# Gate and up matrices of the first block's experts: from 8 KB runs, 1 MiB a transfer, to 16 KB runs, 2 MiB a transfer

## The reference, cut to what matters

```python
def ec_moe(h, router_w, router_b, w_gate, w_up, w_down):
    ...
    gate, idx = lax.top_k(jnp.swapaxes(aff, 1, 2), cap)      # cap = 2 * 256 / 16 = 32
    xg = h[bidx, idx]
    hid = jax.nn.silu(jnp.einsum("becd,edf->becf", xg, w_gate)) * jnp.einsum("becd,edf->becf", xg, w_up)
    y = jnp.einsum("becf,efd->becd", hid, w_down) * gate[..., None].astype(h.dtype)
    return jnp.zeros_like(h).at[bidx, idx].add(y)
```

## Time and profile before

| | |
|---|---|
| profiled execution | 1881.59 us |
| its span | 1879.7 us, mean granted TensorE clock 0.851 |
| PE busy | 1450.5 us (77%), 11264 matmuls |
| PE weight loads busy | 738.8 us (39%) |
| VectorE / ScalarE busy | 432.2 us (23%) / 231.3 us (12%) |
| moved by DMA | 638.02 MB, mean 339 GB/s |
| packets of the queue that SP orders on (q1) | 101040, 623.76 MB |
| gate, up and down transfers | 128 each, 1024 KB, median 18.0, 18.5 and 18.1 us from order to landing |

### The profile page before, as it was taken

How to read it: one execution, slowest core, us unless ns; L and a number is a source line. 1 busy time by engine, 2 the same in 40 slices (tenths; PEclk the granted TensorE clock), 3 DMA queues, 4 the chain that set the end, 5 groups by cost and what they waited for, 6 DMA issues and landing times.

```text
span 1879.7 us, 26140 instructions
## 1 busy us (share of the span) xinstructions
PE 1450.5 (77%) x11264; PEld 738.8 (39%) x11264; DVE 432.2 (23%) x966; ACT 231.3 (12%) x480; POOL 25.7 (1%) x46
## 2 busy tenths in 40 slices
PE   5989866777766667879676666666799985899996
PEld 3834432323332233445332322222246643555553
DVE  1472211104000022534100001000115453311112
ACT  2111100001000020422000000000122232100001
POOL 1000000000000000000000000000020000000000
PEclk8988787878887778888777878787799998899998
DMA  9697999999999983857999999999932302599995
GB/s 376 224 367 301 417 421 421 421 421 421 421 420 422 420 333 112 342 223 300 422 421 421 420 420 422 420 420 422 416 136 82 135 12 101 219 421 420 421 421 224
DMA packets 104811, 638.02 MB, mean 339 GB/s; under 512 B 10524, under 2 KB 10524, under 8 KB 42240
## 3 DMA queue, kind: packets, MB, share of 16 engines
q1 hardware_dynamic: 101040, 623.76, 81.4%
q0 software_dynamic: 3664, 12.64, 1.9%
HBM read 635.30 MB, written 1.96 MB: 339 GB/s over the span
## 4 chain that ended last, share of the span: by engine, by line
DMA 50%; PE 40%; DVE 5%; ACT 2%; issue 1%; SPq 0%; DVEq 0%; ACTq 0%
PE ps L1834 38%; DMA ring<-in_moe_w_up 31%; DMA ring<-in_moe_w_down 16%; DMA ring<-in_ada_w 3%; PE ps L1837 2%; ACT work L2130 1%; DMA ring<-in_moe_w 1%; DVE x L2371 1%; DVE tmp L2369 1%; SPq L280 0%; ACT tmp L2130 0%; ACT hT L2130 0%; ACT xn L2130 0%; DVE work L620 0%; DVE work L617 0%
## 5 line engine op out<-in xcount | busy, mean ns | idle before, releaser
L1834 PE MATMUL ps<-ring,work 128*32 128x256 f32 (+3 forms) x7760 | 821.1, 473 | 300.5 <-DMA ring<-in_moe_w_up 107.5
L1834 PEld LDWEIGHTS ps<-ring,work 128*32 128x32 f32 (+2 forms) x7760 | 339.6, 132 | 761.9 <-issue 219.5
L2130 ACT ACTIVATE work<-ps 128x256 f32<-128x256 f32 (+3 forms) x188 | 89.0, 478 | 1278.7 <-PE ps L1834 1017.0
L1834 PE MATMUL ps<-work 32*128 32x256 f32 (+6 forms) x1034 | 143.2, 467 | 17.4 <-ACT work L2130 15.6
L2504 DVE TENSOR_TENSOR work<-work,ps 128x256 f32<-128x256 f32 x32 | 13.5, 421 | 590.0 <-ACT work L2130 590.0
L1834 PEld LDWEIGHTS ps<-work 32*128 32x128 f32 (+3 forms) x1034 | 86.0, 213 | 72.5 <-issue 50.3
L1834 PE MATMUL ps<-ring,condT 128*32 128x512 f32 x576 | 83.6, 712 | 21.9 <-DMA ring<-in_ada_w 13.7
L1834 PE MATMUL ps<-ring,hT 128*128 128x512 f32 (+1 forms) x224 | 97.1, 597 | 2.4 <-issue 1.3
L1837 PE MATMUL ps<-const,work 128*128 128x128 f32 (+1 forms) x394 | 67.0, 302 | 23.6 <-ACT work L2130 7.3
L1834 PE MATMUL ps<-work,xn 128*128 128x128 f32 (+2 forms) x416 | 69.5, 320 | 7.0 <-DVE work L1672 6.8
L1837 PEld LDWEIGHTS ps<-const,work 128*128 128x128 f32 (+1 forms) x394 | 49.4, 166 | 58.5 <-issue 24.0
(11 more groups left out here) (300 smaller groups left out, 680.9 us busy)
## 6 DMA issues: line engine op xcount, KB each, us to landing
ring<-in_moe_w_gate SPq DMA_DIRECT2D x128, 1024.0 KB, 18.0
ring<-in_moe_w_up SPq DMA_DIRECT2D x128, 1024.0 KB, 18.5
ring<-in_moe_w_down SPq DMA_DIRECT2D x128, 1024.0 KB, 18.1
ring<-in_moe_w SPq DMA_DIRECT2D x102, 1024.0 KB, 10.7
ring<-in_ada_w SPq DMA_DIRECT2D x72, 1024.0 KB, 11.1
ring<-in_w_in SPq DMA_DIRECT2D x10, 1024.0 KB, 18.1
ring<-in_fc_w_in SPq DMA_DIRECT2D x6, 1024.0 KB, 27.1
ring<-in_attn_w_qkv SPq DMA_DIRECT2D x6, 1024.0 KB, 18.2
```

What stands on the lines that cost most here:

```text
L1834: return pe.matmul(out, lhsT, rhs, start=start, stop=stop, skip_group_check=True)
L2130: return nc.scalar.activation(out, in_, f, **kw)
```

## The change

Two gate pieces (or two up pieces) that hold the four rows of the same half become one transfer. It writes both neighbouring slots, 16 KB in one run for each partition, and adds 16 to the semaphore of the first slot alone. An expert's first eight pieces are now two gate pieces, two up, two gate, two up, in place of gate and up by turns. SP waits for the second slot of the pair to be free before it orders. TensorE waits once for a pair, then runs 32 matmuls and still counts `piece_used` after each 16. `loaded` counts only the transfers that really write to a slot's semaphore. The number of matmuls, their shapes and the sum's order of rows stay. Down pieces and all other pieces are as they were.

```diff
+        def second_of_pair(n):
+            return any(n0 <= n < n0 + 12 * E and (n - n0) % 12 in (1, 3, 5, 7) for n0 in (P_MOE_A, P_MOE_B))
         def loaded(pe, n, rounds=0):
-            pe.wait_ge(S(f"loaded{n % SLOTS}"), 16 * (n // SLOTS + 1) + 16 * rounds)
+            transfers = sum(not second_of_pair(m) for m in range(n % SLOTS, n + 1, SLOTS))
+            pe.wait_ge(S(f"loaded{n % SLOTS}"), 16 * (transfers + rounds))
...
+        def pair(n):
+            return ring[:, n % SLOTS:n % SLOTS + 2, :].rearrange("p a (k f) -> p (a k) f", k=2)
+        def load_pair(sp, n, src):
+            sp.dma_start(pair(n), src).then_inc(S(f"loaded{n % SLOTS}"), 16)
...
-                        order = [w[s][:, 0, kp // 2, 2 * (kp % 2):2 * (kp % 2) + 2, :] for kp in range(4) for s in range(2)]
-                        order += [down[:, 0, kp] for kp in range(4)]
-                        for j, src in enumerate(order):
-                            n = n0 + 12 * u + j
+                        for q in range(2):
+                            for s in range(2):
+                                n = n0 + 12 * u + 4 * q + 2 * s
+                                place_free(sp, n + 1, BODY * i)
+                                load_pair(sp, n, w[s][:, 0, q])
+                        for kp in range(4):
+                            n = n0 + 12 * u + 8 + kp
                             place_free(sp, n, BODY * i)
-                            load(sp, n, src)
+                            load(sp, n, down[:, 0, kp])
...
                         for s in range(2):
-                            loaded(pe, n + 2 * kp + s)
-                            w = slot(n + 2 * kp + s).rearrange("p (k f) -> p k f", k=2)
-                            for kk in range(2):
+                            m = n + 4 * q + 2 * s
+                            loaded(pe, m)
+                            for kk in range(4):
                                 for j in range(4):
                                     last = mm(ps[32 * j:32 * j + 32, 4 + s, 0:SEQ],
-                                              xe[:, c % 2, 2 * kp + kk, CAP * u:CAP * u + CAP],
-                                              w[:, kk, SEQ * j:SEQ * j + SEQ],
-                                              kp == 0 and kk == 0, kp == 3 and kk == 1)
-                            last.then_inc(S("piece_used"), 1)
+                                              xe[:, c % 2, 4 * q + kk, CAP * u:CAP * u + CAP],
+                                              pair(m)[:, kk, SEQ * j:SEQ * j + SEQ],
+                                              q == 0 and kk == 0, q == 1 and kk == 3)
+                                if kk % 2:
+                                    last.then_inc(S("piece_used"), 1)
```

More of the change, by code:

```diff
@@ L2053, in experts @@
                         pe.wait_ge(S("spread_ready"), layer * E + e)
-                    for kp in range(4):
-                        if e == 0 and kp == 0:
+                    for q in range(2):
+                        if e == 0 and q == 0:
                             pe.wait_ge(S("xe_dve"), 28 * layer + 4)
-                        if e == 0 and kp == 2:
+                        if e == 0 and q == 1:
                             pe.wait_ge(S("xe_act"), 4 * layer + 4)
-                        if e and u == 0 and kp == 0:
+                        if e and u == 0 and q == 0:
                             pe.wait_ge(S("xe_dve"), 28 * layer + 4 + 8 * c)
                         for s in range(2):
-                            loaded(pe, n + 2 * kp + s)
-                            w = slot(n + 2 * kp + s).rearrange("p (k f) -> p k f", k=2)
-                            for kk in range(2):
+                            m = n + 4 * q + 2 * s
+                            loaded(pe, m)
+                            for kk in range(4):
                                 for j in range(4):
                                     last = mm(ps[32 * j:32 * j + 32, 4 + s, 0:SEQ],
-                                              xe[:, c % 2, 2 * kp + kk, CAP * u:CAP * u + CAP],
-                                              w[:, kk, SEQ * j:SEQ * j + SEQ],
-                                              kp == 0 and kk == 0, kp == 3 and kk == 1)
-                            last.then_inc(S("piece_used"), 1)
+                                              xe[:, c % 2, 4 * q + kk, CAP * u:CAP * u + CAP],
[3 more added lines that the diff above has]
+                                    last.then_inc(S("piece_used"), 1)
                     if e == 1:
```

## The result

The changed kernel takes 1868.78 us (median of 7 runs, 1862.7 to 1870.21). The kernel before takes 1877.36 us beside it (7 runs, 1873.12 to 1882.1). The ratio is 0.9946, 95% interval 0.9932 to 0.9961: a gain of half a per cent, small but clear of the noise. The medians are 8.6 us apart, the ratio says 10.1 us. Forecast were 8.8 us less and 1870.2 us.

A forecast was written before the change was run, and what follows sets the result against it. Both expert stages were taken as bound by one queue's stream of 384 weight transfers of 1 MiB, TensorE waiting. Gain 10.3 - 0.5 (starts) - 1.0 (ends) = 8.8 us, from 1879.0 to 1870.2 us; range 1864.5 to 1880.5.

The forecast's parts named there:

- Part 1, run length: Gate and up stream of both expert stages: 16 KB runs save 82 ns a pair, 10.3 us over 126 pairs.
- The completion packets' 9 ns a pair: Gate and up pairs: one completion packet per DMA engine in place of two, priced at 9 ns a pair.
- Part 2, depth: Weight queue inside the expert stages: later pair orders leave it unbroken, margin 4.4 us, cost 0 us.
- Part 3, the starts: Starts of both expert stages: later pair order costs 0 to 1.5 us in stage B, 0.5 taken; nothing in stage A.
- the second dip: Start of stage B, about 886.5 us: a dip in the stream that the delayed pairs were to fill.
- Part 4, the ends: Ends of both stages: 32 matmuls instead of 16 after the last up landing; 0.5 us lost in each.
- The run isn't 16 KB: Rival, gate and up transfers: the run is cut again at 8 KB; 1879.4 us, chance 0.15 shared with "its length no longer counts".
- its length no longer counts: Rival, gate and up transfers: rate near flat beyond 8 KB runs; 1879.4 us, chance 0.15 shared with "The run isn't 16 KB".
- The fixed time is smaller: Rival, weight stream: a packet's fixed time is smaller, as by the skill's 3 cycles; gain 4.0 - 1.5, 1876.5 us, chance 0.12.
- The dry queue: Rival, after each expert's hidden-state chain: queue runs dry while SP waits for the second down slot; 1889 us, chance 0.06.
- the slow long packet: Rival, gate and up pairs: 16 KB packets slow as in the instruction queue; up to 500 us more, chance 0.04.
- stretches outside them move: Sign, outside the expert stages: if the time there changes, the prediction is wrong; no size given.

The follow-up runs named there:

- experiment 1: The changed kernel's 2 MiB gate and up pairs, but each partition's part in two runs of 8 KB; 1875.7 us, ratio 0.9995 to the kernel before.
- experiment 2: The kernel before, 1 MiB transfers, but gate and up rows taken crosswise in runs of 4 KB, not 8 KB; 1896.5 us, ratio 1.0125 to the kernel before.
- experiment 7: The changed kernel, but each order in the expert stages waits for two more used pieces, as if six slots; 1875.4 us, ratio 0.9999 to the kernel before.
- Experiment 5: The changed kernel, but first and last expert of both stages take gate and up in single 1 MiB transfers; 1868.1 us, ratio 0.9958 to the kernel before.
- kernel 9: The changed kernel itself, unaltered, measured again beside the kernel before; 1868.3 us, ratio 0.9951.
- experiment 8: The changed kernel, but each pair ordered as two 1 MiB transfers of 64 partitions, 16 KB runs kept; 2686.4 us, ratio 1.4157 to the kernel before.

## Why the prediction was right, point by point

**Part 1, run length: right.** 82 ns a pair were forecast, 73 of them for the runs. The stream shows 76 and 67 against the kernel before, 78 and 67 against experiment 1, mean 72; from landing to landing it is 75. Per packet the step from 4 to 8 KB was read as 9.1 ns; experiment 2 gives 8.8 to 9.3 for that step, the changed kernel against experiment 1 gives 9.0 to 9.4 for the step to 16 KB. The completion packets' 9 ns a pair are not there: experiment 1 has 2048 fewer, and its 4 MiB take the same 9.94 to 9.95 us. The forecast of 10.3 us stands against 9.4 us between the changed kernel's stages and experiment 1's.

**Part 2, depth: right, too cautious.** No gap opened; in experiment 7, with six slots in place of eight, a stage under way lost 0.7 to 1.0 us.

**Part 3, the starts: right place, size off.** 0.5 us taken, between 0 and 1.5; by the bytes it is 1.0 us (0.42 MB not moved before the first matmul of stage B). I thought that the delayed pairs would fill the second dip. The dip was too shallow for that: in the earlier trace rows its four slices, 0.325 us each, are 7, 7, 5 and 7 tenths busy, which leaves some 0.4 us idle (an estimate from that row) for a delay of 1.5 us.

**Part 4, the ends: wrong sign.** A cost of 1.0 us was taken for both. Stage A's end is unchanged at 12.8 us, so the waits cover the second half of the pair there. Stage B's is 1.8 us shorter, since the last down piece and the scatter ran at full clock (1342.03 follows a block of 64 matmuls without a wait; in the earlier trace rows the last 16 took 1.94 us). The prediction reckoned that the pieces behind the pair might fall to the half clock, not that the pair might keep them at the full one. Experiment 5 takes the pair away from the end and gets the 14.6 us back, and the other profiles agree.

**The sum.** 10.3 - 0.5 - 1.0 = 8.8; the stages show 8.5 us, the medians 8.6, the ratios of two measurements 10.1 and 9.2. The main term is right, but that the sum comes within 0.3 us is luck. By place, the 8.5 us are 8.4 in the two streams, 1.8 gained at the end of stage B and 1.8 lost before expert 1's first landing, its offset of one piece taken off (0.1 in stage A, 1.7 in B; 0.8 and 1.2 in kernel 9). The forecast had 9.7 us for the 118 pairs of the streams, 1.0 lost at the ends, and before expert 1's first landing a gain of 0.2 (0.7 from eight pairs, less 0.5 for the starts). These terms are off by 1.2, 2.8 and 2.0 us, and the errors cancel. The absolute forecast is 1.4 us high, because it was made from the first three runs' median (1879.0), which lies 1.65 us over that of seven.

**The rivals.** "The run isn't 16 KB" fell with the packet count, "its length no longer counts" with 425 GB/s against experiment 1's 421. "The fixed time is smaller" fell with experiments 1 and 2. The dry queue had no trace, and the slow long packet neither: 8 MiB at 16 KB and 4 MiB at 8 KB give 425 GB/s as the model said. One of my signs was wrong: "stretches outside them move" was to show the prediction wrong, but they move by some us between any two kernels.

## What to carry to other kernels

Where a stream of full-width transfers already runs without a gap, the number of packets is what changed its rate here: take the step between two run lengths in your own trace (here 73 ns for eight packets) and carry it one doubling further. Making transfers of 1 MiB larger brought nothing by itself, and it costs where the ring is being refilled, since an order then waits for its last slot. Measure such a change between two landings inside the stage, best by the median over many such stretches; the whole span hides 5 us under parts that have nothing to do with it.

## What the runs showed that was not expected

Pairs raise TensorE's granted clock. Over each kernel's timed runs its mean is 0.864 in the changed kernel, 0.864 in experiment 1, and 0.873 to 0.874 with down in pairs too, against 0.846 to 0.848 for the kernel before beside them. In the windows above the same matmuls take less PE time: 291.6 us busy in 460 at a clock of 0.86, where the kernel before has 318.8 at 0.80. What the engine did before: 32 matmuls in a row behind a wait of 1 to 4 us, in place of 16 behind 0.5 to 1.6. It bought nothing inside the stages, since TensorE waits for the stream there, and experiment 1 has the clock without the gain. The one place where it was seen to pay is the end of stage B, where TensorE's own work is what is left: the 1.8 us of experiment 5.

Transfers of 64 partitions, one after the other to either half, ran at 236 GB/s where 128 partitions gave 425 (experiment 8).
